# One encoder layer on one core: seam work moved between phases, scan copies placed earlier, one attention product put ahead of a barrier

## The chip, the cores and the metric

The kernel runs on one core of a Trainium2 chip (trn2). The metric is the device time of one execution in microseconds, as a median of runs. One further execution is profiled; all rows below are from it.

## The reference, cut to what matters

One layer over 1024 tokens of width 1024, in float32:

```python
h = h + 0.5 * swiglu(rmsnorm(h, ffn1_norm), w_gate, w_up, w_down)      # D_FF = 2816
n = rmsnorm(h, mix_norm); z = n @ w_in       # c_q 256 | c_kv 128 | k_rope 32 | u 512 | g_attn 1024 | g_ssm 1024
attn = mla_attention(...)                    # 8 heads, 64 + 32 rotary dims, latents c_q and c_kv, softmax over 1024 keys
ssm  = glu(gelu(s5_forward(u) + s5_backward(u) + d * u))               # 32 groups, 64 complex states, both directions
h = h + (sigmoid(g_attn) * (attn @ w_o_attn) + sigmoid(g_ssm) * (ssm @ w_o_ssm)) @ w_out
h = h + 0.5 * swiglu(rmsnorm(h, ffn2_norm), w2_gate, w2_up, w2_down)
out = rmsnorm(h, final_norm)
```

## The kernel before, in words

Each float32 operand of a large product is split into a rounded high part and a low rest, and each product is three matmul passes (high by high, high by low, low by high: lines 48 to 50, `three_passes`). So nearly every weight tile costs a cast on ScalarE (`high`) and a subtraction on VectorE or GpSimd (`low`) before TensorE can use it. The program is written out by hand: in each phase every engine has its own block of instructions in a fixed order, with explicit semaphore waits, and between two phases stands a barrier of all engines at which the old phase's semaphores are cleared (line 69). All DMAs of these phases are issued by SyncE and go through one queue (q1).

The phases, in order, are: first FFN, input projection, `ssm_phase`, `mixer_phase`, `merge_phase`, second FFN.

**The FFNs** (`ffn_phase`). The products are computed with seven block products in place of eight (`PRODUCTS`), so both the normalised rows and the weights are first combined into sums. The start of the phase, for matrix 0: TensorE turns the low rows (`turn_lows`, line 1314), makes `first_product` (0,0), then (0,2), turns the sums of one tile (`turn_sums`), makes `first_product` (1,0), turns the next sums, and so on, then goes on with product q = 1 of matrix 0. `T[i]`, the sums of rows, are made by GpSimd (`combine`, four instructions a tile), the weight sums `S` as well (`sums`, line 1300). `low` (line 1036) is VectorE's half of a weight block, `lows_low` and `sums_low` (lines 1065 and 1070) its halves of the turned rows, `normalised(i)` the root mean square of two tiles (`norm.var`, `norm.inverse`: five small instructions, lines 98 to 102) and the scaling of these tiles (line 1052). In the second FFN the first four tiles come normalised from the merge (`ahead=QUAD`); the other four are squared, stored to `kept` and normalised here. The first FFN has the same code without that head start.

**`ssm_phase`.** VectorE runs a serial scan of 127 steps, three small instructions each (lines 1758 to 1762). Beside it TensorE makes thirteen gate products `side.gp.product(pe, n)`, 48 matmuls each. `side.sigmoid(act, n)` reads the result of product n (line 1587), frees its PSUM banks, and casts the weights of product n + 2 (`gp.high(act, n + 2)`, line 165), from which GpSimd makes the low part (line 173), without which product n + 2 does not start. When the scan is over, `forward(b)` copies states on ScalarE (line 1711, two copies each) and `backward(b)` on VectorE, and TensorE makes the output product of block 0 (line 1683). ScalarE's order is:

```python
def forward(b):
    if b == 0:
        act.wait_ge(s["scan"], CH)          # the last step of the scan
...
for n in range(GATES_FIRST - 1):            # GATES_FIRST = 13
    side.sigmoid(act, n)
forward(0)
forward(1)
side.sigmoid(act, GATES_FIRST - 1)
```

**`mixer_phase`.** Eight products of the GLU (`glu.product(pe, n)`), after each of which one latent tile is turned (`latent(n)`, read by ScalarE and VectorE, lines 2112 and 2219), then the first head's projection (`project(0, x)`, which waits for all eight latents), then eight products with `w_o_ssm` (`wos.product`), after each of which one value tile is made (`value(n)`); then the loop over heads. VectorE evicts `wos` product n with line 2265; TensorE's product n + 2 waits for that. The last work of the heads is GpSimd's `aT_lo` (line 2330).

**`merge_phase`.** Eight products `woa.product(pe, n)` with `w_o_attn`, 24 matmuls each. VectorE's line 2466 multiplies product n with its gate tile (512 KB, loaded by line 2412 from DRAM), and product n + 2 waits for this read. SyncE issues gate 0, partial 0, weights 3, gate 1, partial 1, weights 4, then the 4 MB of `kept` (line 2416), and then, each after VectorE's sum n - 2, gate n, partial n and the next weights. Sixteen units with `w_out` follow, and at the end four residual additions by VectorE (line 2402).

Of the kernel before, what the change touches and what calls it, by code (L numbers as in the profile page):

```python
# [32 lines left out]
P = 128  # L33
# [662 lines left out]
def ffn_map(base):  # L696
# [5 lines left out]
    return where, total  # L702


def ffn_phase(nc, tag, gain, w_gate, w_up, w_down, rows, ident, psum, hidden, residual, x=None, finish=None, tables=None, ahead=0, following=None, loaded=None):
# [10 lines left out]
    with Phase(nc) as ctx:  # L716
# [6 lines left out]
        stat = sb("stat", [P, 5, ST])  # L723
        B_hi, B_lo = (at(n, [P, PRODUCTS, KH, HALF], F32R, n) for n in ("B_hi", "B_lo"))
        A_hi, A_lo = (at(n, [P, PRODUCTS, KH, P], F32R, n) for n in ("A_hi", "A_lo"))
        raw, gb = loaded or ([at(f"raw{j}", [P, KT, 2 * P], F32, "raw", 8 * KB * j) for j in range(2)], at("gb", [P, D], F32, "ring"))
        S = at("S", [P, 4, KH, P], F32, "S")
# [33 lines left out]
        s_kept = [sem(f"kept{m}") for m in range(ST if x is None else 0)]  # L761
# [22 lines left out]
        low_turned = lambda m, i: QUAD * i + m + 1  # L784
        arrived = lambda n: 32 * (n // 2 + (0 if loaded else 1))
# [13 lines left out]
        def _(sp):  # L799
# [17 lines left out]
            def take(m):  # L817
                if m < ahead:
                    return
                if x is not None:  # L820
                    sp.dma_start(rows[:, m, :], x[m * P:(m + 1) * P, :]).then_inc(s_x[m], 16)
                else:
                    sp.dma_start(residual[m * P:(m + 1) * P, :], rows[:, m, :]).then_inc(s_kept[m], 16)
# [68 lines left out]
        def _(act):  # L892
            def square(m):
                if x is not None:
                    act.wait_ge(s_x[m], 16)
                if m > ahead:
                    act.wait_ge(s_sq, m - ahead)
                act.activation(dump[:], rows[:, m, :], ACT.Square, accum_out=stat[:, 0, m:m + 1]).then_inc(s_sq, 1)  # L898

            def squares(i):  # L900
                square(2 * i)
                square(2 * i + 1)
                norm.root(act, i - ahead // 2, slice(2 * i, 2 * i + 2))
# [6 lines left out]
            def sums_high(m):  # L910
                if m == 0:
                    act.wait_ge(s_sq, ST - ahead)
# [8 lines left out]
            def high(n, q):  # L921
# [7 lines left out]
                if summed:  # L929
                    act.wait_ge(s_sum, 4 * n + summed)  # L930
                elif arrived(n):
# [50 lines left out]
            if not loaded:  # L982
                high(0, 0)
            squares(2)
# [3 lines left out]
            squares(3)  # L988
            high(1, 0)
            high(1, 2)  # L990
            sums_high(0)
# [4 lines left out]
            for q in (1, 3, 4, 5, 6):  # L996
# [42 lines left out]
        def _(dve):  # L1039
            def rstd(i):  # L1040
                norm.inverse(dve, i - ahead // 2, slice(2 * i, 2 * i + 2))

            def variance(i):
                dve.wait_ge(s_sq, 2 * i + 2 - ahead)
                norm.var(dve, i - ahead // 2, slice(2 * i, 2 * i + 2))

            def scaled(m):
                if m == 0:
                    dve.wait_ge(s_gain, 16)
                if x is None:  # L1050
# [49 lines left out]
            if not loaded:  # L1100
# [9 lines left out]
            for q in (1, 3, 4, 5, 6):  # L1110
# [164 lines left out]
        def _(pool):  # L1275
# [13 lines left out]
            def sums(n, part=slice(0, 4)):  # L1289
# [4 lines left out]
                for i, (a, b, op, q) in list(enumerate(((A21, A22, ALU.add, 4), (S[:, 0], A11, ALU.subtract, 1),  # L1294
# [3 lines left out]
                    if i in (1, 3):  # L1298
                        pool.wait_ge(s_sum, 4 * n + (1 if i == 1 else 2))
                    pool.tensor_tensor(S[:, i], a, b, op).then_inc(s_sum, 1)  # L1300

            sums(0)
# [296 lines left out]
def ssm_phase(nc, w, rows, rows_at, ident, psum, nT_hi, nT_lo, u, gates, kern_dram, C_dram, lam8_dram):  # L1599
# [5 lines left out]
    with Phase(nc) as ctx:  # L1605
# [83 lines left out]
        def _(act):  # L1689
# [29 lines left out]
            forward(0)  # L1719
            forward(1)  # L1720
# [871 lines left out]
```

## Time and profile before

| | us |
|---|---|
| median of 3 runs | 2269.32 |
| lowest, highest | 2269.16, 2269.6 |
| the profiled execution, its own time | 2267.31 |
| its span in the profile | 2265.5 |

TensorE was busy for 2144.2 us of the span (95%), VectorE for 1473.9, ScalarE for 916.9, GpSimd for 610.1. The granted TensorE clock was 0.982 of full speed in the mean: 1.00 is the level of 2.4 GHz, 0.50 that of 1.2 GHz. A time in a row of the timeline is counted from the start of the span. What stands in square brackets at the end of a row is the idle time of the engine before it, and who ended it.

### The profile page before, as it was taken

The page shows a single profiled execution, that of the slowest core. Times are in us where ns is not written, and L with a number is a line of the kernel's source. Part 1 is how long each engine was busy: PE and PEld are TensorE (multiplying, and loading weights), DVE is VectorE, ACT ScalarE, POOL GpSimd, SP SyncE. Part 2 cuts the span into 40 slices and gives each one's busy share as a digit, 9 for nine tenths or more (in the row PEclk, how much of TensorE's full clock was granted, in tenths as well). Part 3 has the DMA queues.
Part 4 walks back from the last instruction along what each step waited for, and adds up shares of the span by engine and source line. Part 5 has one row for each costly group of instructions (what it writes and reads, how often), then busy time and mean ns, then how long its engine had stood idle before and what let it go on. Part 6 is the DMA issues. An engine that isn't in the chain of part 4 may idle for free. (4 is left out here: it accounts for less than half of the span.)

```text
span 2265.5 us, 27670 instructions
## 1 busy us (share of the span) xinstructions
PE 2144.2 (95%) x10074; PEld 1779.3 (79%) x10074; DVE 1473.9 (65%) x2306; ACT 916.9 (40%) x1552; POOL 610.1 (27%) x510
## 2 busy tenths in 40 slices
PE   5899999999999899999999999899799999999997
PEld 4678888887887798878777887687678888887886
DVE  7786667657777524992447887454766565657777
ACT  5423333323445234225427778422533323324444
POOL 5337777750000003220002333100633333310000
PEclk9999999999999899999999999999899999999999
DMA  3433333349333427331340000362123232349333
GB/s 121 108 90 114 126 118 123 118 160 342 117 98 116 139 80 163 98 89 57 112 140 16 7 7 15 140 234 105 56 88 122 89 121 89 121 142 356 100 96 110
DMA packets 234471, 263.00 MB, mean 116 GB/s; under 512 B 34720, under 2 KB 169376, under 8 KB 233824
## 3 DMA queue, kind: packets, MB, share of 16 engines
q1 hardware_dynamic: 234336, 261.23, 36.4%
q8 instruction: 81, 1.33, 0.2%
q14 instruction: 54, 0.44, 0.1%
HBM read 184.60 MB, written 76.58 MB: 115 GB/s over the span
## 5 line engine op out<-in xcount | busy, mean ns | idle before, releaser
L48 PE MATMUL psum<-f_B_hi,f_A_hi 128*128 128x512 f32 x1232 | 489.8, 398 | 32.2 <-DVE f_A_lo L1036 23.7
L49 PE MATMUL psum<-f_B_lo,f_A_hi 128*128 128x512 f32 x1232 | 484.5, 393 | 0.0
L50 PE MATMUL psum<-f_B_hi,f_A_lo 128*128 128x512 f32 x1232 | 484.2, 393 | 0.0
L48 PEld LDWEIGHTS psum<-f_B_hi,f_A_hi 128*128 128x128 f32 x1232 | 234.2, 190 | 84.9 <-DVE f_A_lo L1036 27.5
L50 PEld LDWEIGHTS psum<-f_B_hi,f_A_lo 128*128 128x128 f32 x1232 | 234.2, 190 | 49.8
L49 PEld LDWEIGHTS psum<-f_B_lo,f_A_hi 128*128 128x128 f32 x1232 | 234.4, 190 | 47.6
L1300 POOL TENSOR_TENSOR f_S<-f_raw 128x512 f32<-128x512 f32 x88 | 134.7, 1531 | 445.5 <-DVE f_A_lo L1036 289.7
L933 ACT CAST f_A_hi<-f_S 128x512 fp32r<-128x512 f32 x176 | 109.2, 623 | 351.5 <-PE psum L50 347.1
L48 PE MATMUL psum<-f_wd,f_hh 128*128 128x512 f32 x616 | 240.4, 390 | 3.6 <-DVE f_wd L1082 3.6
L49 PE MATMUL psum<-f_wd,f_hh 128*128 128x512 f32 x616 | 240.4, 390 | 0.0
L50 PE MATMUL psum<-f_wd,f_hh 128*128 128x512 f32 x616 | 240.2, 390 | 0.0
L967 ACT CAST f_hh<-f_h_raw 128x512 fp32r<-128x512 f32 x154 | 96.0, 624 | 240.4 <-PE psum L50 231.7
L1036 DVE TENSOR_TENSOR f_A_lo<-f_raw,f_A_hi 128x512 fp32r<-128x512 f32 x132 | 132.4, 1004 | 70.1 <-ACT f_A_hi L933 69.4
L1080 DVE TENSOR_TENSOR f_hh<-f_h_raw,f_hh 128x512 fp32r<-128x512 f32 x154 | 106.6, 692 | 104.9 <-ACT f_hh L967 104.1
L1036 DVE TENSOR_TENSOR f_A_lo<-f_S,f_A_hi 128x512 fp32r<-128x512 f32 x176 | 138.7, 790 | 1.3 <-ACT f_A_hi L933 0.2
L933 ACT CAST f_A_hi<-f_raw 128x512 fp32r<-128x512 f32 x132 | 81.9, 620 | 142.1 <-PE psum L50 130.2
L48 PEld LDWEIGHTS psum<-f_wd,f_hh 128*128 128x128 f32 x616 | 116.0, 188 | 28.7 <-DVE f_wd L1082 4.4
L50 PEld LDWEIGHTS psum<-f_wd,f_hh 128*128 128x128 f32 x616 | 116.0, 188 | 24.2
L49 PEld LDWEIGHTS psum<-f_wd,f_hh 128*128 128x128 f32 x616 | 115.9, 188 | 23.9
L2211 DVE TENSOR_TENSOR mx_PT_lo<-psum,mx_PT_hi 128x512 fp32r<-128x512 f32 x128 | 87.8, 686 | 47.2 <-ACT mx_PT_hi L2076 46.8
L1737 POOL TENSOR_TENSOR u<-u,ss_C_mat 128x512 f32<-128x512 f32 x8 | 9.9, 1273 | 356.7 <-DMA ss_C_mat<-ssm_d 356.7
L1082 DVE TENSOR_TENSOR f_wd<-f_wd_raw,f_wd 128x512 fp32r<-128x512 f32 x154 | 105.7, 686 | 0.0
(327 smaller groups left out, 4277.3 us busy)
## 6 DMA issues: line engine op xcount, KB each, us to landing
f_h_raw<-hidden SPq DMA_DIRECT2D x154, 256.0 KB, 2.6
hidden<-rows SPq DMA_DIRECT2D x44, 768.0 KB, 4.6
f_raw<-ffn_w_gate SPq DMA_DIRECT2D x44, 512.0 KB, 5.1
f_raw<-ffn_w_up SPq DMA_DIRECT2D x44, 512.0 KB, 5.1
f_wd_raw<-ffn_w_down SPq DMA_DIRECT2D x44, 512.0 KB, 9.2
rows<-x SPq DMA_DIRECT2D x16, 512.0 KB, 7.3
ga_raw<-w_in SPq DMA_DIRECT2D x16, 512.0 KB, 4.3
gates<-ga_sig SPq DMA_DIRECT2D x32, 256.0 KB, 2.2
```

Source lines behind the costliest of these rows:

```text
L48: pe.matmul(out, lhs_hi, rhs_hi, start=first, stop=False, skip_group_check=go_on)
L49: pe.matmul(out, lhs_hi, rhs_lo, start=False, stop=False, skip_group_check=go_on)
L50: return pe.matmul(out, lhs_lo, rhs_hi, start=False, stop=last, skip_group_check=go_on)
L933: act.copy(A_hi[:, q], src).then_inc(s_hi, 1)
L967: act.copy(hh[v % 2][0][:], h_raw[v % 8][:]).then_inc(s_dhi, 1)
L1036: eng.tensor_tensor(A_lo[:, q], src, A_hi[:, q].bitcast(F32), ALU.subtract).then_inc(s_lo, 1)
L1080: dve.tensor_tensor(hh[v % 2][1][:], h_raw[v % 8][:], hh[v % 2][0][:].bitcast(F32), ALU.subtract).then_inc(s_dlo, 1)
L1082: dve.tensor_tensor(wd[v % 2][1][:], wd_of(q, k), wd[v % 2][0][:].bitcast(F32), ALU.subtract).then_inc(s_dlo, 1)
L1300: pool.tensor_tensor(S[:, i], a, b, op).then_inc(s_sum, 1)
L1737: pool.tensor_tensor(u[:, g], u[:, g], Db[:, g].unsqueeze(2).broadcast_to([P, 4, T, SG]), ALU.mult).then_inc(s["ud"], 1)
L2211: dve.tensor_tensor(pt(PT_lo, g, x), turned_bank(x), pt(PT_hi, g, x).bitcast(F32), ALU.subtract).then_inc(s["tr_lo"], 1)
```

## The change

It has five parts.

1. `ssm_phase`: on ScalarE `forward(0)` and `forward(1)` stand after `side.sigmoid(act, 8)` in place of after `side.sigmoid(act, 11)`. What `forward(0)` waits for is the same.
2. `mixer_phase`: latent 1 is turned together with latent 0 after GLU product 0, and each later one a product sooner, the last after product 6; ScalarE and VectorE take a pair of latents directly after the sigmoid, ahead of the casts of the weights and of the wait for the next product. The value tiles are moved in the same way.
3. `woa.product(pe, 0)` is the last work of TensorE in `mixer_phase`, where it waits for the parts of `aT_lo` as it needs them; `merge_phase` starts with product 1.
4. The squares of tiles 4 to 6, the stores of tiles 4 to 7 and the four weight sums of matrix 0 are made in `merge_phase`. The second FFN squares tile 7 alone, normalises the four tiles with one chain of small instructions and scales tiles 6 and 7 later.
5. In both FFNs `high(0, 1)` and `low(0, 1)` stand ahead of the sums' halves (`sums_high`, `sums_low`) in place of behind them.

The diff, cut to its core:

```diff
 # ffn_phase, ScalarE
-            squares(2)
+            if loaded:
+                square(ST - 1)
+                norm.root(act, 0, slice(QUAD, ST))
+            else: ...
             lows_high(1)
             high(0, 2)
             first_copy(0)
-            squares(3)
+            if not loaded:
+                squares(3)
             high(1, 0)
             high(1, 2)
+            high(0, 1)
             sums_high(0)
...
-            for q in (1, 3, 4, 5, 6):
+            for q in (3, 4, 5, 6):
                 high(0, q)
 # ffn_phase, VectorE
-            normalised(2)
+            if loaded:
+                dve.wait_ge(s_sq, SQUARES)
+                norm.var(dve, 0, slice(QUAD, ST))
+                norm.inverse(dve, 0, slice(QUAD, ST))
+                scaled(QUAD)
+                scaled(QUAD + 1)
...
             lows_low(1)
             low(0, 2)
-            normalised(3)
+            if loaded:
+                scaled(QUAD + 2)
+                scaled(QUAD + 3)
...
             low(1, 0)
             low(1, 2)
+            low(0, 1)
             for m in range(QUAD):
                 sums_low(m)
 # ffn_phase, GpSimd
-            sums(0)
+            if not loaded:
+                sums(0)
 # ssm_phase, ScalarE
             for n in range(GATES_FIRST - 1):
                 side.sigmoid(act, n)
-            forward(0)
-            forward(1)
+                if n == GATES_FIRST - 5:
+                    forward(0)
+                    forward(1)
             side.sigmoid(act, GATES_FIRST - 1)
 # mixer_phase
+        def sooner(n):
+            return (0, 1) if n == 0 else (n + 1,) if n + 1 < ST else ()
...
             for n in range(glu.N):
                 glu.product(pe, n, (lambda k: pe.wait_ge(s_lo, 2 * k + 2)) if n == 0 else None)
-                latent(n)
+                for m in sooner(n):
+                    latent(m)
...
                 wos.product(pe, n, (lambda k: pe.wait_ge(s_vlo, k + 1)) if n == 0 else None)
-                value(n)
+                for m in sooner(n):
+                    value(m)
...
+            pe.wait_ge(s["exp"], G)
+            woa.product(pe, 0, lambda k: pe.wait_ge(s["av_lo"], 4 * k + 4))
 # merge_phase, SyncE, ScalarE, GpSimd, TensorE
-            sp.wait_ge(s_next, 64)
+            for i in range(QUAD):
+                sp.wait_ge(s_add, QUAD + i + 1)
+                sp.dma_start(kept[(QUAD + i) * P:(QUAD + i + 1) * P, :], rows[:, QUAD + i, :]).then_inc(s_keep[QUAD + i], 16)
...
+            for m in range(QUAD, ST - 1):
+                act.wait_ge(s_add, m + 1)
+                act.wait_ge(s_sq, m)
+                act.activation(dump[:], rows[:, m, :], ACT.Square, accum_out=next_stat[:, 0, m:m + 1]).then_inc(s_sq, 1)
...
+            pool.wait_ge(s_next[0], 32)
+            pool.tensor_tensor(next_S[:, 0], A21, A22, ALU.add).then_inc(s_nsum, 1)
...
-            for n in range(KT):
+            for n in range(1, KT):
                 woa.product(pe, n)
```

How the instructions stand now, at three places. The first is ScalarE in `ssm_phase`, around the copies of states (`rows<-ss_H`); a row `ga_sig` is one sigmoid, `ga_hi` the cast of the weights of the product after the next. Before:

```order
L165 CAST ga_hi<-ga_raw 128x1024
L1587 ACTIVATE ga_sig<-psum 128x512 x2
L165 CAST ga_hi<-ga_raw 128x1024
L1711 COPY rows<-ss_H 64x128x8 x4
L1587 ACTIVATE ga_sig<-psum 128x512 x2
L165 CAST ga_hi<-ga_raw 128x1024
L1711 COPY rows<-ss_H 64x128x8 x2
```

And of the changed kernel, on the same engine:

```order
L165 CAST ga_hi<-ga_raw 128x1024
L1731 COPY rows<-ss_H 64x128x8 x4
L1607 ACTIVATE ga_sig<-psum 128x512 x2
L165 CAST ga_hi<-ga_raw 128x1024
L1607 ACTIVATE ga_sig<-psum 128x512 x2
L165 CAST ga_hi<-ga_raw 128x1024
L1607 ACTIVATE ga_sig<-psum 128x512 x2
L165 CAST ga_hi<-ga_raw 128x1024
L1607 ACTIVATE ga_sig<-psum 128x512 x2
L165 CAST ga_hi<-ga_raw 128x1024
L1731 COPY rows<-ss_H 64x128x8 x2
```

The four copies of blocks 0 and 1 stood one sigmoid and one cast ahead of the next two copies, and now stand four of each ahead of them.

The second place is the end of `mixer_phase` on TensorE (the branches are the end of one phase's block and the start of the next one's; `mx_PT_lo,mx_V` is the last product of the heads). Before:

```order
L1987 MATMUL psum<-mx_PT_hi,mx_V 128x512
L1988 MATMUL psum<-mx_PT_lo,mx_V 128x512
L1792 UNCONDITIONAL_BRANCH
L2497 UNCONDITIONAL_BRANCH
L48 MATMUL psum<-aT_hi,woa_hi 128x512
```

And of the changed kernel, with the first and the last of the product's 24 matmuls:

```order
L2012 MATMUL psum<-mx_PT_hi,mx_V 128x512
L2013 MATMUL psum<-mx_PT_lo,mx_V 128x512
L48 MATMUL psum<-aT_hi,woa_hi 128x512
...
L50 MATMUL psum<-aT_hi,woa_lo 128x512
L1813 UNCONDITIONAL_BRANCH
L2549 UNCONDITIONAL_BRANCH
L48 MATMUL psum<-aT_hi,woa_hi 128x512
```

Product 0 stands ahead of the branches, so ahead of the barrier.

The third place is VectorE at the start of the second FFN. Before, from the halves of the first turned rows on:

```order
L1065 TENSOR_TENSOR f_B_lo<-psum,f_B_hi 128x4x128 x4
L1036 TENSOR_TENSOR f_A_lo<-f_raw_15743,f_A_hi 128x512
L368 TENSOR_SCALAR f_stat<-f_stat 128x2
L98 RECIPROCAL f_stat<-f_stat 128x2
L99 TENSOR_TENSOR f_stat<-f_stat 128x2
L100 TENSOR_TENSOR f_stat<-f_stat 128x2
L101 TENSOR_SCALAR f_stat<-f_stat 128x2
L102 TENSOR_TENSOR f_stat<-f_stat 128x2
L1052 SCALAR_TENSOR_TENSOR rows<-rows,f_stat,f_gb 128x1024 x2
L1036 TENSOR_TENSOR f_A_lo<-f_raw_15744,f_A_hi 128x512 x2
L1070 TENSOR_TENSOR f_B_lo<-psum,f_B_hi 128x4x128 x20
L1036 TENSOR_TENSOR f_A_lo<-f_S,f_A_hi 128x512 x3
```

And of the changed kernel, the same stretch:

```order
L1073 TENSOR_TENSOR f_B_lo<-psum,f_B_hi 128x4x128 x4
L1044 TENSOR_TENSOR f_A_lo<-f_raw_15774,f_A_hi 128x512
L1060 SCALAR_TENSOR_TENSOR rows<-rows,f_stat,f_gb 128x1024 x2
L1044 TENSOR_TENSOR f_A_lo<-f_raw_15775,f_A_hi 128x512 x2
L1044 TENSOR_TENSOR f_A_lo<-f_S,f_A_hi 128x512
L1078 TENSOR_TENSOR f_B_lo<-psum,f_B_hi 128x4x128 x20
L1044 TENSOR_TENSOR f_A_lo<-f_S,f_A_hi 128x512 x2
```

The second chain of small instructions is gone (one chain of twice the width stands earlier), and one half of the weight sums has moved ahead of the twenty halves of the turned sums.

## Rows read from the trace of the kernel before

**Rows 1.** The page, part 1: busy time, share of the span, instructions.

```profile
PE 2144.2 (95%) x10074; PEld 1779.3 (79%) x10074; DVE 1473.9 (65%) x2306; ACT 916.9 (40%) x1552; POOL 610.1 (27%) x510
```

**Rows 2.** Timeline of ScalarE in `ssm_phase`: start us, us, instruction, idle before it.

```profile
972.54 1.05 ACT L165 CAST ga_hi<-ga_raw 128x1024 fp32r<-128x1024 f32 x1
982.45 1.09 ACT L1587 ACTIVATE ga_sig<-psum 128x512 f32<-128x512 f32 x2 [8.86 <-PE psum L50]
...
993.33 1.09 ACT L1587 ACTIVATE ga_sig<-psum 128x512 f32<-128x512 f32 x2 [8.86 <-PE psum L50]
...
1015.00 7.40 ACT L1711 COPY rows<-ss_H 64x1024 f32<-64x1024 f32 x4 [8.77 <-DVE ss_H L1762]
...
1023.21 1.03 ACT L165 CAST ga_hi<-ga_raw 128x1024 fp32r<-128x1024 f32 x1
```

**Rows 3.** Timelines of GpSimd and VectorE in `ssm_phase`.

```profile
1024.32 2.41 POOL L173 TENSOR_TENSOR ga_lo<-ga_raw,ga_hi 128x1024 fp32r<-128x1024 f32 x1 [15.61 <-ACT ga_hi L165]
984.64 2.38 DVE L1762 TENSOR_TENSOR ss_H<-ss_H,ss_prod 128x64 f32<-128x64 f32 x1
...
1014.74 0.22 DVE L1762 TENSOR_TENSOR ss_H<-ss_H,ss_prod 128x64 f32<-128x64 f32 x1
```

**Rows 4.** Timeline of TensorE, the output products of blocks 0 and 1.

```profile
1018.92 5.44 PE L1683 MATMUL psum<-ss_C_mat,rows 128*128 128x128 f32 x32 [3.87 <-ACT rows L1711]
...
1035.12 3.73 PE L1683 MATMUL psum<-ss_C_mat,rows 128*128 128x128 f32 x32
```

**Rows 5.** Timelines of TensorE, VectorE and ScalarE in `mixer_phase`, ahead of the heads.

```profile
1132.47 0.79 PE L48 MATMUL psum<-mx_lT_hi,mx_w_hi 128*128 128x512 f32 x1 [4.21 <-DVE mx_lT_lo L2219]
...
1189.83 0.47 PE L48 MATMUL psum<-mx_KT_hi,mx_QT_hi 96*128 96x512 f32 x1 [1.49 <-DVE mx_V L2223]
1130.25 1.22 DVE L2246 TENSOR_TENSOR mx_sT_lo<-mx_val,mx_sT_hi 128x1024 fp32r<-128x1024 f32 x1 [1.11 <-ACT mx_sT_hi L2137]
...
1162.20 1.23 DVE L2265 TENSOR_TENSOR mx_out<-psum,mx_gate 128x1024 f32<-128x1024 f32 x1
...
1135.43 0.59 ACT L2058 ACTIVATE mx_qf<-psum 64x512 f32<-64x512 f32 x1 [3.66 <-PE psum L50]
```

**Rows 6.** Timelines of GpSimd, TensorE, SyncE's queue and VectorE around the merge's start.

```profile
1448.65 1.26 POOL L2330 TENSOR_TENSOR aT_lo<-mx_att,aT_hi 64x512 fp32r<-64x512 f32 x1 [0.81 <-ACT aT_hi L2107]
1451.14 0.77 PE L48 MATMUL psum<-aT_hi,woa_hi 128*128 128x512 f32 x1 [6.12 <-PEq L69]
1454.02 0.54 SPq L2416 DMA_DIRECT2D rows<-kept  x1
1461.77 0.33 SPq L2412 DMA_DIRECT2D mg_gate<-gates  x1
...
1473.63 1.23 DVE L2466 TENSOR_TENSOR mg_val<-psum,mg_gate 128x1024 f32<-128x1024 f32 x1 [4.72 <-DMA mg_gate<-gates]
```

**Rows 7.** Windows there: us, busy of each engine, granted clock, DMA share, GB/s.

```profile
1451.14:1456.25 5.11, 5.11 (x12) 4.05 (x13) 0.00 (x0) 0.00 (x0) 0.00 (x0) 0.50 0.79 263
1462.00:1473.20 11.20, 11.20 (x51) 9.29 (x50) 4.53 (x5) 2.50 (x3) 0.00 (x0) 1.00 1.03 405
```

**Rows 8.** Timelines of TensorE and VectorE at the second FFN's start.

```profile
1598.77 0.79 PE L48 MATMUL psum<-f_B_hi,f_A_hi 128*128 128x512 f32 x1 [4.91 <-DVE f_A_lo L1036]
1610.29 0.79 PE L48 MATMUL psum<-f_B_hi,f_A_hi 128*128 128x512 f32 x1 [4.35 <-DVE f_A_lo L1036]
1627.45 0.80 PE L48 MATMUL psum<-f_B_hi,f_A_hi 128*128 128x512 f32 x1 [2.87 <-DVE f_A_lo L1036]
1604.99 3.58 DVE L1052 SCALAR_TENSOR_TENSOR rows<-rows,f_stat,f_gb 128x1024 f32<-128x1024 f32 x2
...
1626.71 1.89 DVE L1036 TENSOR_TENSOR f_A_lo<-f_S,f_A_hi 128x512 fp32r<-128x512 f32 x3
```

**Rows 9.** TensorE at the first FFN's start; ScalarE's square there in the second.

```profile
59.23 0.50 PE L48 MATMUL psum<-f_B_hi,f_A_hi 128*128 128x512 f32 x1 [2.87 <-DVE f_A_lo L1036]
1589.11 1.09 ACT L898 ACTIVATE f_dump<-rows 128x1024 f32<-128x1024 f32 x1
```

More of the change, by code:

```diff
@@ L760, in ffn_phase @@
         s_gain, s_sq, s_xn, s_T, s_tr, s_bhi, s_blo = map(sem, ("gain", "sq", "xn", "T", "tr", "bhi", "blo"))
-        s_kept = [sem(f"kept{m}") for m in range(ST if x is None else 0)]
+        if loaded:
+            ctx.taken += loaded[4].taken
+        s_kept = loaded[5] if loaded else None
+        SQUARES = 1 if loaded else ST
         s_raw = [sem(f"raw_in{j}") for j in range(2)]
@@ L895, in square @@
                     act.wait_ge(s_x[m], 16)
-                if m > ahead:
-                    act.wait_ge(s_sq, m - ahead)
+                if m and not loaded:
+                    act.wait_ge(s_sq, m)
                 act.activation(dump[:], rows[:, m, :], ACT.Square, accum_out=stat[:, 0, m:m + 1]).then_inc(s_sq, 1)
@@ L902, in squares @@
                 square(2 * i + 1)
-                norm.root(act, i - ahead // 2, slice(2 * i, 2 * i + 2))
+                norm.root(act, i, slice(2 * i, 2 * i + 2))
             def lows_high(i):
@@ L928, in high @@
                     act.wait_ge(s_tr, ALL_TURNED)
-                if summed:
-                    act.wait_ge(s_sum, 4 * n + summed)
-                elif arrived(n):
+                if summed and sums_done(n, summed):
+                    act.wait_ge(s_sum, sums_done(n, summed))
+                elif not summed and arrived(n):
                     act.wait_ge(s_raw[j], arrived(n))
@@ L981, in _ @@
             lows_high(0)
-            if not loaded:
+            if loaded:
+                square(ST - 1)
+                norm.root(act, 0, slice(QUAD, ST))
+            else:
                 high(0, 0)
-            squares(2)
+                squares(2)
             lows_high(1)
@@ L2150, in _ @@
                         queries(0, x)
-                value(n)
+                for m in sooner(n):
+                    value(m)
             split(1)
@@ L2266, in _ @@
                 wos.low(dve, n + 3)
-                value(n)
+                for m in sooner(n):
+                    value(m)
                 if n == 1:
@@ L2552, in build @@
         where, _ = ffn_map(-(-nc.sbuf_base // 32) * 32)
+        stores = Taken()
         loaded = ([nc.alloc_sbuf_tensor_at(f"f2_raw{j}", [P, KT, 2 * P], F32, offset=where["raw"] + 8 * 1024 * j) for j in range(2)],
-                  nc.alloc_sbuf_tensor_at("f2_gb", [P, D], F32, offset=where["ring"]))
+                  nc.alloc_sbuf_tensor_at("f2_gb", [P, D], F32, offset=where["ring"]),
+                  nc.alloc_sbuf_tensor_at("f2_S", [P, 4, KH, P], F32, offset=where["S"]),
+                  nc.alloc_sbuf_tensor_at("f2_stat", [P, 5, ST], F32, offset=where["stat"]),
+                  stores, [semaphores(nc, stores, "keep")(f"tile{m}") for m in range(ST)])
         merge_phase(nc, w, psum, rows, kept, woa, held, loaded, gates, partial, w["ffn2_norm"][0])
```

59 lines of the change are left out of this document (38 added, 21 removed).

## The prediction

> **What bounds the kernel now.** First the page's busy times: TensorE is busy for 95% of the span [rows 1], so only what shortens one of its waits, or a stretch at the low clock, can make the kernel faster, and any new wait of TensorE is paid in full. So next I listed TensorE's waits in the timeline, and for each the engine that ended it. The five parts of the change aim at six of them: 3.87 us at the scan's end [rows 4], 4.21 and 1.49 us in the mixer [rows 5], 6.12 us at the merge's start [rows 6], and 4.91, 4.35 and 2.87 us at the second FFN's start [rows 8], with a 2.87 us wait in the first FFN that is like the last of these [rows 9]. After each of the longer ones TensorE restarts at half clock: 5.11 us at 0.50 behind the 6.12 us wait [rows 7], first matmuls of 0.79 us behind the others [rows 5, 8]. At half clock half of the time is lost, 2.55 us in the first case; in the mixer the six matmuls of the first projection took 1135.43 - 1132.47 = 2.96 us [rows 5] where six at full clock take 1.36 (48 take 993.33 - 982.45 = 10.88 us [rows 2]), so 1.6. For a restart that I can't place I take 2.3 us, a little outside these two as bounds: 1.5 to 2.9.
>
> **Part 1, the scan's copies: a wait that blocks ScalarE.** The copies wait for the scan's last step, which ends at 1014.96 [rows 3], and the copies' row says so: 8.77 us idle, ended by VectorE's `ss_H` [rows 2]. They are not held up by the sigmoids ahead of them; ScalarE is idle there. In the new order ScalarE comes to them after the cast of 972.54 [rows 2] and stands still until the scan is over. Behind it is queued sigmoid 9, at 982.45 before, and its cast. That cast makes the weights of product 11, and sigmoid 9 frees the banks that product 11 writes. Product 10 still runs, as its cast is the one of 972.54. It ends where the sigmoid of 993.33 begins [rows 2], and there TensorE stops.
>
> How long it stops: the scan itself gets shorter, since GpSimd's subtraction blocks one step of it each time: a step's instruction that takes 0.22 us takes 2.38 beside GpSimd's 2.4 [rows 3]. Three of these subtractions (those behind the sigmoids 9, 10 and 11) now come after the scan: 3 x 2.16 = 6.5 us, so it ends at 1008.5. The copies take 7.40 [rows 2], to 1015.9. From the copies' end (1022.40) to the end of GpSimd's next low part (1024.32 + 2.41 = 1026.73) it is 4.33 us [rows 2, 3]; by the same steps product 11 starts at 1020.2. TensorE is idle for 1020.2 - 993.3 = 26.9 us, and restarts at half clock, 2.3 more. Then the products 11 and 12 run back to back, as before; the copies are long done, so the 3.87 us wait is gone, and the output product of block 0 runs at full clock (3.73 in place of 5.44, 1.7 less [rows 4]). Sum: 26.9 + 2.3 - 3.87 - 1.7 = **+23.6 us** (bounds 22 to 25: the restart's, and one blocked step more or less).
>
> **Part 2, latents and values.** Latent 7 is now turned before the last GLU product and read while that runs, so the projection starts where the product ends: the 4.21 us go, and with them the half clock (1.6). TensorE is then 5.8 us earlier. What is late next is ScalarE's read of the projection (1135.43 before): it waits also for VectorE's last `sT_lo`, whose end stays at 1131.47, so it comes 3.9 us sooner and not 5.8. From it a chain over VectorE's rotary instructions, the eviction of `wos` product 0, a weight load, ScalarE's queries and a value leads to the eviction of 1162.20 [rows 5], for which product 4 waits; it moves by the same 3.9, and TensorE waits about 2 us there. The 1.49 us wait for the last value goes too, as that value stands before the last product now, and so does a little of its three matmuls (0.7 us) from behind it: 3.9 + 1.49 + 0.3 = **-5.7 us** (bounds -3.9, the chain alone, and -7.3, all of 4.21, 1.6 and 1.49).
>
> **Part 3, the attention product.** Its 24 matmuls take 5.44 us at full clock (half of 10.88 [rows 2]). 18 of them need parts of `aT_lo` that are there, and run in the idle stretch that begins at 1451.14 - 6.12 = 1445.02. The last six wait for GpSimd's 1448.65 + 1.26 = 1449.91 [rows 6] and end at about 1451.45. The barrier took 1.23 us from 1449.91 to 1451.14; it now ends at about 1452.7, so everything that SyncE issues for the merge is 1.55 us later. TensorE has product 0 behind it and no half clock, and runs products 1 to 3 (3 x 5.44) until 1469.05. Before, it reached product 4 at 1451.14 + 4 x 5.44 + 2.55 = 1475.45. But product 4 waits for VectorE's read of product 2, which waits for gate 2, and this landed only just before 1473.63, issued at 1461.77: 4.72 us of idle, ended by the DMA [rows 6]. Ahead of it in the queue stand the 4 MB of `kept`, issued at 1454.02; the DMA engines are full from then on (share 1.03 at 405 GB/s [rows 7]). A faster TensorE does not make these bytes come sooner, and they start 1.55 us later. So VectorE's read is at 1475.2 to 1476.4, and TensorE waits from 1469.05 to 1476.4, 7.4 us, then restarts at half clock (2.3). Against 1475.45 that is 0.95 + 2.3 = **+3.2 us** (bounds 2.4 to 3.9, the restart's), and products 5 to 7 follow.
>
> The Trainium skill, DMA: Bandwidth & Descriptors, section Queues, rings and completion order, says that descriptors are consumed in ring order on each DMA engine, but that completion is not first in, first out per issuing engine. If gate 2 could overtake `kept`, part 3 would give what its idle time promises (the second rival). Here the trace is for the order of issue: gate 2 came 19.6 us after `kept` was issued and not before it.
>
> **Part 4, the second FFN's start.** The stores in the merge add a last DMA issue behind the last addition, 0.33 to 0.54 us of SyncE [rows 6], to the barrier: +0.4. The squares of tiles 4 to 6 run beside the additions of the next tiles, the weight sums on GpSimd beside the units, at no cost (if they were not hidden, one square, 1.09 [rows 9]). At the start one square is gone from the chain to the first wait and VectorE no longer meets GpSimd's sums: 4.91 becomes 3.9, -1.0. In the second wait, TensorE stood for VectorE's second norm: from 1598.7 to 1608.57, ahead of `low(1, 0)` [rows 8]. Now two scalings alone stand there, at most 3.58, while TensorE makes product (0,2) and turns a tile for over 7 us: the 4.35 us go, and the half clock behind them (1.5, the low bound, as turns of rows follow soon). In the third wait `low(0, 1)` is ready, so TensorE need not wait for one of the three in 1.89 us [rows 8], nor for the last of the twenty halves, as long again, which product q = 1 does not read: -1.2. Sum 0.4 - 1.0 - 4.35 - 1.5 - 1.2 = **-7.6 us**. What is late next is GpSimd's row sums, four tiles in series. Bounds: -4.5, if those hold the third turn up by 3 us, and -10, if a restart or two keeps the full clock.
>
> **Part 5, the first FFN.** The same 1.2 us of the wait of 59.23 [rows 9]: **-1.2 us** (bounds 0 and -2.9, with the half clock behind it).
>
> **Sum.** 23.6 - 5.7 + 3.2 - 7.6 - 1.2 = +12.3 us. The profiled execution took 2267.31 by its own clock, 1.8 around a span of 2265.5, and would take 2279.6. It lies 2.0 below the median of 2269.32, to which I add the same: **2281.6 us**.
>
> **The rivals.**
> *The scan's wait costs nothing* (other side, faster). If the scan were over when ScalarE comes to the copies, the copies would lie in its idle time (8.86 us beside each product [rows 2]), and part 1 would give -3.87 - 1.7 = -5.6. Sum -16.9: 2252.4. The point from which part 1 decides the sign: its cost must be under 11.3, so the scan must end 12.3 us earlier than 1008.5, at 996. VectorE's rows show no such slack; for it is only that part 1 was meant so. 0.03.
> *`kept` does not bind.* Then TensorE keeps part 3's gain: 5.44 of product 0 and 2.55 of half clock, less 1.55: -6.4 in place of +3.2. 2272.0. For it is that the queue might serve small loads sooner, against it the row of the gate. 0.07.
> *The row sums bind at the second FFN.* GpSimd's instructions and VectorE's meet more than before, as the scalings and three halvings stand in one run; part 4 gives its low bound or less, -3: 2286.2. 0.12.
> My forecast, all five parts within their bounds: 0.78.
>
> **How the numbers follow.** Faster than before by over 0.2% (4.5 us; about what a measurement of this kernel tells from no change) is below 2264.8, slower is above 2273.8. Faster needs the first rival: 0.03, and 0.01 for a sum of mistakes. Within lie the second rival and the low tail of the forecast, 0.08. Slower: 0.88. The bounds of the five terms, added in squares about the sum, are some 4 us to either side; the low end goes further, to take in most of what the second rival leaves out: 2275.5 to 2287.
>
> **What the changed profile would show.** Right: a wait of TensorE of about 27 us in `ssm_phase` ahead of product 11, released by `ga_lo`, and ScalarE idle for some 35 us ahead of the copies, released by `ss_H`; no wait ahead of the first projection, but one of about 2 us ahead of a `wos` product; a new wait of about 7 us among the `woa` products, ended by VectorE's `mg_val` that itself waits for the gate's DMA, with clock 0.50 behind it; of the waits at the second FFN's start one of about 3.9 us, and none of 4.35. Wrong would be: copies that run before 1000 us, or products 11 and 12 without a wait; product 4 of the merge before 1475; a first product q = 1 of the second FFN over 38 us after its phase's start (now 40.95, predicted 33).

## The result and the profile after

| | before | changed |
|---|---|---|
| median, 5 runs each | 2269.6 us | 2280.84 us |
| lowest, highest | 2269.16, 2271.57 | 2280.62, 2282.77 |
| the profiled execution, and its span | 2267.31, 2265.5 | 2280.62, 2278.6 |

The ratio is 1.005, with a 95% interval of 1.0038 to 1.0063: the change makes the kernel 11 us slower, where 12.3 were forecast. By the two spans it is 13.1 us.

The page of the changed kernel, part 1 (busy us, share of the span, instructions), answers to [rows 1]:

```profile
PE 2140.6 (94%) x10074; PEld 1775.5 (78%) x10074; DVE 1469.8 (65%) x2300; ACT 916.9 (40%) x1551; POOL 610.9 (27%) x510
```

TensorE is busy for 3.6 us less in a span that is 13.1 longer: it waits 16.7 us more. To find the place, the program is cut at the first instruction of TensorE in each stage, as the timeline gives its start, and the differences are taken (us); the mixer's stage is cut once more, at the first matmul of the heads' scores (`mx_KT`, `mx_QT`). Each row is one profiled execution. The experiments stand in the same table; what each of them is follows below.

| kernel | first FFN | projection | `ssm_phase` | mixer up to the first scores | heads and merge | second FFN |
|---|---|---|---|---|---|---|
| before | 729.4 | 114.1 | 228.8 | 117.6 | 396.7 | 679.0 |
| changed | 725.7 | 114.3 | 253.1 | 111.8 | 402.8 | 670.9 |
| 1: copies back | 724.9 | 114.0 | 228.7 | 111.9 | 402.6 | 672.5 |
| 2: product 0 back | 726.0 | 115.1 | 252.4 | 111.5 | 399.2 | 670.9 |
| 3: `kept` split | 724.8 | 114.3 | 253.0 | 112.0 | 393.1 | 671.0 |
| 4: split, product 0 back | 726.1 | 114.3 | 251.7 | 113.4 | 399.6 | 672.5 |
| 5: copies and latents back | 725.1 | 114.3 | 228.7 | 117.6 | 401.7 | 670.9 |
| 6: FFN parts only | 725.6 | 114.3 | 228.7 | 117.6 | 400.5 | 672.5 |
| 7: part 5 only | 727.4 | 115.2 | 230.0 | 118.0 | 399.4 | 680.8 |
| 8: three edits | 724.9 | 114.0 | 225.7 | 111.9 | 393.1 | 671.0 |
| 9: later subtraction | 725.7 | 113.9 | 225.8 | 111.8 | 402.3 | 672.5 |
| 10: still later | 725.3 | 115.5 | 226.7 | 113.4 | 402.3 | 671.0 |
| 11: three edits, still later | 724.6 | 115.5 | 225.1 | 112.0 | 393.2 | 670.9 |

`ssm_phase` takes 24.3 us more, the heads and the merge 6.1 more; the mixer's start takes 5.8 less, the second FFN 8.1 less, the first 3.7 less, in these two executions. A stage with the same code can differ by 2 to 3 us between two executions: heads and merge, which experiment 7 leaves alone, took 399.4 us there against 396.7 before. Now the places themselves. Timelines of the changed kernel in `ssm_phase` (start us, us, what; in brackets the idle time before): ScalarE, then VectorE, GpSimd and TensorE. They answer to [rows 2 to 4].

```profile
969.09 1.06 ACT L165 CAST ga_hi<-ga_raw 128x1024 fp32r<-128x1024 f32 x1
1005.11 7.34 ACT L1731 COPY rows<-ss_H 64x1024 f32<-64x1024 f32 x4 [34.97 <-DVE ss_H L1783]
1012.26 1.10 ACT L1607 ACTIVATE ga_sig<-psum 128x512 f32<-128x512 f32 x2
1013.25 1.03 ACT L165 CAST ga_hi<-ga_raw 128x1024 fp32r<-128x1024 f32 x1
...
1004.85 0.23 DVE L1783 TENSOR_TENSOR ss_H<-ss_H,ss_prod 128x64 f32<-128x64 f32 x1
...
1014.36 2.34 POOL L173 TENSOR_TENSOR ga_lo<-ga_raw,ga_hi 128x1024 fp32r<-128x1024 f32 x1 [41.73 <-ACT ga_hi L165]
...
1016.75 0.79 PE L48 MATMUL psum<-nT_hi,ga_hi 128*128 128x512 f32 x1 [26.91 <-POOL ga_lo L173]
...
1041.50 3.73 PE L1703 MATMUL psum<-ss_C_mat,rows 128*128 128x128 f32 x32
```

The chain is read from bottom to top. Product 11 waits 26.91 us for GpSimd's low part. This waited for ScalarE's cast of 1013.25, and the cast stood behind the copies. Ahead of the copies ScalarE was idle for 34.97 us, until the scan's last step, which ends at 1005.08. The phase itself starts 3.45 us earlier than in the kernel before; counted from there, the step ends at what would be 1008.5 in that kernel's rows. Block 0's output product now runs without a wait and at full clock.

TensorE and VectorE of the changed kernel in the mixer, against [rows 5]:

```profile
1180.99 0.47 PE L48 MATMUL psum<-mx_sT_hi,wos_hi 128*128 128x512 f32 x1 [2.76 <-DVE mx_out L2295]
...
1179.62 1.23 DVE L2295 TENSOR_TENSOR mx_out<-psum,mx_gate 128x1024 f32<-128x1024 f32 x1
```

The 4.21 and 1.49 us waits are gone; `wos` product 4 waits 2.76 us. TensorE, SyncE and VectorE at the merge's start, against [rows 6], then three windows against [rows 7], the first in the last head (us, busy of PE, PEld, DVE, ACT and POOL, granted clock, DMA share, GB/s):

```profile
1466.91 0.50 PE L48 MATMUL psum<-aT_hi,woa_hi 128*128 128x512 f32 x1 [0.90 <-POOL aT_lo L2361]
...
1469.76 0.47 PE L48 MATMUL psum<-aT_hi,woa_hi 128*128 128x512 f32 x1 [1.20 <-PEq L69]
...
1494.21 0.76 PE L48 MATMUL psum<-aT_hi,woa_hi 128*128 128x512 f32 x1 [7.84 <-DVE mg_val L2518]
...
1472.57 0.53 SPq L2447 DMA_DIRECT2D rows<-kept  x1
1475.92 1.14 SPq L2443 DMA_DIRECT2D mg_gate<-gates  x1
...
1481.27 6.17 SPq L2444 DMA_DIRECT2D mg_part<-partial  x1
...
1492.84 1.23 DVE L2518 TENSOR_TENSOR mg_val<-psum,mg_gate 128x1024 f32<-128x1024 f32 x1 [10.22 <-DMA mg_gate<-gates]
```
```profile
1456.39:1459.80 3.41, 3.41 (x12) 2.48 (x11) 0.00 (x0) 0.17 (x1) 1.31 (x2) 0.50 0.00 0
1472.60:1492.80 20.20, 13.77 (x61) 11.07 (x59) 7.33 (x7) 3.25 (x4) 0.00 (x0) 0.94 1.02 385
1494.21:1497.35 3.14, 3.14 (x8) 2.46 (x9) 3.14 (x4) 1.57 (x2) 0.00 (x0) 0.50 1.06 376
```

The wait of 6.12 us is 1.20, and one of 7.84 stands ahead of product 4. Gate 2, issued 3.35 us behind `kept`, let VectorE go on at 1492.84, 16.9 us after its issue, with the DMA engines full in between (share 1.02). Counted from the issue of `kept`, VectorE could read the gate after 20.3 us. In all nine profiles with one load of `kept` this took 18.9 to 20.3 us, whether gate 2 was issued 3.4 us behind `kept` (product 0 ahead of the barrier) or 6.8 to 8.1 us (product 0 behind it): to issue the gate sooner does not bring it sooner. The second FFN's start, TensorE and VectorE, against [rows 8], and TensorE in the first FFN, against [rows 9]:

```profile
1607.71 3.69 PE L1334 MATMUL psum<-ident,rows 128*128 128x128 f32 x32 [2.94 <-PEq L69]
...
1618.49 0.79 PE L48 MATMUL psum<-f_B_hi,f_A_hi 128*128 128x512 f32 x1 [3.89 <-DVE f_A_lo L1044]
...
1641.18 0.47 PE L48 MATMUL psum<-f_B_hi,f_A_hi 128*128 128x512 f32 x1 [1.19 <-DVE f_B_lo L1078]
...
1645.87 0.47 PE L48 MATMUL psum<-f_B_hi,f_A_hi 128*128 128x512 f32 x1 [1.72 <-DVE rows L1140]
...
1618.35 4.52 DVE L1060 SCALAR_TENSOR_TENSOR rows<-rows,f_stat,f_gb 128x1024 f32<-128x1024 f32 x2
...
58.22 0.47 PE L48 MATMUL psum<-f_B_hi,f_A_hi 128*128 128x512 f32 x1 [1.76 <-DVE f_B_lo L1078]
...
62.91 0.47 PE L48 MATMUL psum<-f_B_hi,f_A_hi 128*128 128x512 f32 x1 [1.68 <-DVE rows L1140]
```

The first product with q = 1 starts 33.5 us after the phase's first instruction (before 40.9). Of the three waits 3.89, none and 1.19 are left. A new one of 0.52 us, for GpSimd's row sums, stands ahead of the last turn of the sums, at 1639.34.

### The profile page after: what moved, and what is told of

Same layout as the page of the kernel before. It is cut to its first block and busy times, and to the rows that moved or that the text cites. A ratio compares the mean times of both kernels' runs of the same rounds, so it can differ in the third digit from the quotient of the medians.

```text
span 2278.6 us, 27668 instructions
## 1 busy us (share of the span) xinstructions
PE 2140.6 (94%) x10074; PEld 1775.5 (78%) x10074; DVE 1469.8 (65%) x2300; ACT 916.9 (40%) x1551; POOL 610.9 (27%) x510
## 5 line engine op out<-in xcount | busy, mean ns | idle before, releaser
L1319 POOL TENSOR_TENSOR f_S<-f_raw 128x512 f32<-128x512 f32 x86 | 129.2, 1502 | 302.8 <-DVE f_A_lo L1044 282.5
L48 PE MATMUL psum<-nT_hi,ga_hi 128*128 128x512 f32 x256 | 101.4, 396 | 27.8 <-POOL ga_lo L173 26.9
```

The source lines that it names most:

```text
L48: pe.matmul(out, lhs_hi, rhs_hi, start=first, stop=False, skip_group_check=go_on)
```

## The experiments

Each table row above is one profiled execution, and not always the one nearest to the median; the medians below are of 4 to 12 runs, each beside runs of the kernel before on the same chip, whose median was 2270.29 for the experiments 1 to 4, 2272.94 for 5 to 8 and 2271.83 for 9 to 11 (17, 17 and 11 runs). These three medians differ by up to 2.7 us with one and the same kernel, and the changed kernel was not run beside them. So a difference from its 2280.84, or between experiments of different groups, can be off by as much; the ratios and the stages don't depend on that. All but 7 start from the changed kernel.

**1. Part 1 undone.**

```diff
-                if n == GATES_FIRST - 5:
-                    forward(0)
-                    forward(1)
+            forward(0)
+            forward(1)
             side.sigmoid(act, GATES_FIRST - 1)
```

> The changed kernel with part 1 undone: the four copies of the scan's states stand behind sigmoid 11 again. Theory (the copies' wait for the scan blocks ScalarE, and this costs 26.9 of idle TensorE and 2.8 of restart, less the 3.87 wait and 1.6 of half clock that went): 24.3 us less than the changed kernel's 2280.84, so 2256.5, with a wait of about 3.9 ahead of the output product of block 0 and none ahead of product 11. Rival (the wait of 26.9 comes mostly from the earlier start of the phase and from what stands before it, and the place of the copies moves only the last 3.87): 2277 to 2285.

Measured: 2258.01 us (2256.59 to 2259.25), ratio 0.9946 (0.9933 to 0.9958). `ssm_phase` took 228.7 us in place of 253.1, what it took before; the wait ahead of block 0 is back, with a restart at half clock (5.44 in place of 3.73), and ahead of product 11 there is none. TensorE's timeline:

```profile
1014.25 5.44 PE L1703 MATMUL psum<-ss_C_mat,rows 128*128 128x128 f32 x32 [3.87 <-ACT rows L1731]
```

The place of two lines, the copies, costs 24.4 us, and it alone decides the sign of the change. The rival had 2277 to 2285 and is out.

**2. Product 0 back in the merge** (`woa.product(pe, 0, ...)` out of the heads' block, `for n in range(KT)` in the merge).

> The changed kernel with the first attention output product back in the merge, behind the barrier. Theory (product 0 ahead of the barrier makes everything that SyncE issues later, and gate 2 behind the 4 MB of kept sets the time of product 4): 3.4 us less than 2280.84, so 2277.4; 2275.7 if the half clock of the last head goes too; a wait of 6 at the barrier and none ahead of product 4. Rival (product 0 ahead saves its 5.44 and the half clock behind the barrier, and the 7.84 wait has nothing to do with it): 6.4 us more, 2287.2.

Measured: 2277.04 us (2275.71 to 2279.65), ratio 1.0031 (1.0019 to 1.0044). Heads and merge took 399.2, 3.6 less than with part 3. The barrier's wait is back, and ahead of product 4 there is none:

```profile
1467.95 0.76 PE L48 MATMUL psum<-aT_hi,woa_hi 128*128 128x512 f32 x1 [6.12 <-PEq L69]
```

The rival's 2287.2 is out. The last head has its half clock here too, so product 0 is not its cause.

**3. The load of `kept` in 8 pieces.** VectorE waits for the first four ahead of the first additions and for the others ahead of the last.

```diff
-                if n == 1:
-                    sp.dma_start(rows[:], kept.rearrange("(m p) d -> p m d", p=P)).then_inc(s_kept, 16)
+                if n >= QUAD:
+                    back(sp, n - QUAD)       # one tile of 512 KB
...
                 if 3 <= u < 7:
+                    back(sp, u + 1)
```

> The changed kernel with the 4 MB load of kept cut into 8 loads of 512 KB, one each behind the gates 4 to 7 and the weights of units 3 to 6, in place of one load behind gate 1. Theory (gate 2 lands late only because 4 MB stand ahead of it): the 7.84 us wait ahead of product 4 and the restart behind it, 2.4, go: 10.2 us less than 2280.84, so 2270.6, and gate 2 lands within 5 us of its issue. Rival (the DMA engines are the limit, whatever the order, as the same bytes must be moved in the same stretch): the wait stands a little later, 2279 to 2282.

Measured: 2270.95 us (2269.39 to 2273.59), ratio 1.0005 (0.9996 to 1.0014). TensorE has no wait between the barrier's and the end of the products. SyncE's queue and VectorE's reads of the products 2 and 3, and a window:

```profile
1475.06 0.32 SPq L2446 DMA_DIRECT2D mg_gate<-gates  x1
...
1480.99 1.23 DVE L2522 TENSOR_TENSOR mg_val<-psum,mg_gate 128x1024 f32<-128x1024 f32 x1 [0.64 <-DMA mg_gate<-gates]
1485.46 1.23 DVE L2522 TENSOR_TENSOR mg_val<-psum,mg_gate 128x1024 f32<-128x1024 f32 x1 [0.15 <-PE psum L50]
```
```profile
1472.00:1485.00 13.00, 13.00 (x59) 10.78 (x58) 11.22 (x11) 4.82 (x6) 0.00 (x0) 1.00 1.04 373
```

The DMA engines are as full as in the changed kernel (share 1.04 and 1.02), so the rival's premise holds, but its conclusion doesn't: the gate is read 5.9 us after its issue (within 5 was expected) in place of 16.9, because less stands ahead of it. Heads and merge took 393.1 in place of 402.8, 9.7 less.

**4. Both.**

> Both edits: product 0 back in the merge and kept in 8 loads. Theory (without product 0 ahead, gate 2 was in time by 1.8 us, so kept cost nothing there): the same as with product 0 back alone, 2277.4 (or 2275.7), so product 0 ahead of the barrier is worth 5 to 7 us once kept is out of its way, and costs 3.4 when it is not. Rival (kept slows other transfers of the merge in both cases): some 5 us less than with product 0 back alone, near 2271.

Measured: 2277.07 us (2275.69 to 2279.49), ratio 1.0029 (1.0018 to 1.0041), the same as experiment 2: without product 0 ahead, splitting `kept` gives nothing, and the rival (near 2271) is out. So the two edits are worth something only together: product 0 ahead costs 3.6 us behind the one load (402.8 - 399.2) and gives 6.5 behind the split one (399.6 - 393.1). The 3.6 are of one pair of executions: with one load of `kept`, the five profiles with product 0 ahead have 401.7 to 402.8 for the stage and the four experiments without it (2, 6 and 7, and 4 with its split load) 399.2 to 400.5, in the mean some 2.6 less.

**5. Parts 1 and 2 undone** (latents and values behind the product with their own number again).

> The changed kernel without the parts 1 and 2: copies behind sigmoid 11, latents and values at their old places; parts 3, 4 and 5 stay. Theory (part 2 is worth 5.7 us, and 5.8 by the marks of the two profiles): 2258.0, measured without part 1 alone, plus 5.7: 2263.7, with the 4.21 and 1.49 us waits back in the mixer. Rival (the half clock in the last head, 3.4 us long, which the kernel before does not have, comes from part 2 and takes 1.6 of its gain): 2262.1, and no half clock there.

Measured: 2263.61 us (2260.23 to 2266.01), ratio 0.9969 (0.9954 to 0.9984): 5.7 over experiment 1 by the stage (117.6 against 111.9), and 5.2 by the two ratios. The half clock in the last head is there without part 2, so the rival falls.

**6. Parts 1, 2 and 3 undone.**

> The changed kernel without the parts 1, 2 and 3: only what changes the two FFNs, their loads, stores, squares and weight sums. Theory (part 3 costs 3.4 us; the parts 4 and 5 give 7.3 and 3.4 by the marks): 2259 to 2260.5. Rival (the first FFN gives only the 1.2 us of one wait, the rest of its 3.4 was a difference of two executions): 2261.5 to 2263.

Measured: 2261.06 us (2257.43 to 2261.83), ratio 0.9948 (0.9936 to 0.996). Beside experiment 5, on the same chip, part 3 costs 2.6 us. The median lies 8.5 below the 2269.6 of the first table, and 11.9 below the runs of the kernel before beside it; the forecast for both FFN parts was 8.8. The two readings differ by more than theory (2259 to 2260.5) and rival (2261.5 to 2263), and the median lies between them, so this run doesn't tell them apart.

**7. Part 5 alone, on the kernel before** (it changes both FFNs).

```diff
             high(1, 2)
+            high(0, 1)
             sums_high(0)
...
-            for q in (1, 3, 4, 5, 6):
+            for q in (3, 4, 5, 6):
```

> The kernel before with one edit: in both FFNs matrix q = 1 is split directly behind (1, 2), ahead of the sums of tiles and weights. Theory (1.2 us of each of two waits of 2.87): 2.4 us less than before, 2267.2, and of the waits 1.7 is left. Rival (the first FFN's 3.4 us by the marks are this edit's): 3.4 there and 1.2 to 3.4 in the second, 2263 to 2265.

Measured: 2268.23 us (2264.14 to 2272.6, 12 runs), ratio 0.9984 (0.9974 to 0.9993): by the ratio 3.6 us less, with an interval of 1.6 to 5.9, and by the medians 4.7. The theory's 2.4 lies in the interval, and so does the near end of the rival's 4.6 to 6.8, so the size stays open. Both waits of 2.87 are 1.76. TensorE's timeline in the second FFN, which took 680.8 us against 679.0 all the same, as it has 6.8 us more at half clock in this execution (the slowest of the twelve):

```profile
1630.93 0.47 PE L48 MATMUL psum<-f_B_hi,f_A_hi 128*128 128x512 f32 x1 [1.76 <-DVE f_B_lo L1071]
```

Experiment 6 differs from this kernel by part 4 alone. On the same chip it is 7.2 us faster by the medians and 8.2 by the ratios; the forecast for part 4 without the 1.2 us of its third wait, which both kernels have, was 6.4.

**8. Three edits:** copies back, `kept` split, and GpSimd's subtraction for product 13 behind the scan.

```diff
             for n in range(1, side.N):
+                if n == GATES_FIRST:
+                    pool.wait_ge(s["scan"], CH)
                 side.gp.low(pool, n)
```

> The changed kernel with three edits: the copies behind sigmoid 11 again, kept in 8 loads, and GpSimd's subtraction for product 13 behind the scan's last step in place of beside it. Theory: 2258.0 measured without part 1, less 9.7 (the wait of 7.29 ahead of product 4 and a restart of 2.4), less 2.2 (one step of the scan no longer takes 2.4 in place of 0.22, so the scan ends 2.2 sooner and the wait of 3.87 ahead of block 0 becomes 1.7): 2246.1. Rival (the subtraction behind the scan comes too late for product 13, or VectorE's copies of the states meet it): no gain from this edit, 2248.3, or a new wait ahead of product 13, 2250.

Measured: 2251.83 us (2242.57 to 2252.19), ratio 0.9905 (0.989 to 0.9921). The five runs lie in two groups, 2242.57 and 2245.45, and three at 2251.83 to 2252.19: the median misses the 2246.1 of the theory, and the rival's 2248.3 as well. The profile is of the fastest run, so what the slower three have more is not shown. In it the wait ahead of block 0 was not 1.7 but 2.54. VectorE and GpSimd behind the scan:

```profile
1008.28 6.86 DVE L1791 COPY rows<-ss_H 64x1024 f32<-64x1024 f32 x4
...
1008.33 3.36 POOL L173 TENSOR_TENSOR ga_lo<-ga_raw,ga_hi 128x1024 fp32r<-128x1024 f32 x1 [15.12 <-DVE ss_H L1784]
```

VectorE's four copies took 6.86 us in place of 4.31, and the subtraction 3.36 in place of 2.4. The collision was moved, not removed, as the rival had it, though it took 0.8 of the expected 2.2 us and not all. The Trainium skill, SBUF — State Buffer, section Who interferes with whom, says that copies can lock the port pair that VectorE shares with GpSimd, and that the one that comes second stands still until the other's instruction is over; by it each loses about one instruction of the other, and the rows agree with 2.5 and 1.0 us.

**9 and 10. The subtraction behind the scan, and behind VectorE's copies** (`pool.wait_ge(s["bw"], 4)` in place of the wait above), both with the copies back and one load of `kept`.

> The copies behind sigmoid 11 again, and GpSimd's subtraction for product 13 waits for the scan's last step; kept is one load. Against the copies back alone (2258.0) theory says: the wait ahead of block 0 is 2.5 in place of 3.87, as in the run with all three edits, where the subtraction then ran beside VectorE's copies of the states and made four of them take 6.87 in place of 4.36; and the half clock behind this wait goes, 1.7: 3.0 less, 2255.0. Rival (the half clock was gone by chance of the execution): 1.3 less and the half clock is there, 2256.7.

> As the run before, but GpSimd's subtraction waits for VectorE's four copies of the states too. Theory (an instruction of VectorE that reads and writes SBUF takes longer beside GpSimd's): the four copies take 4.4 again, ScalarE's first two are then what block 0 waits for, 1.7 in place of 2.5, and product 13 is not late, as the subtraction ends near 1015.1 and product 13 starts near 1016.0: 0.8 less than the run before, 2254.2. Rival (product 13 waits for the subtraction): a new wait of 1 to 2 there, and no gain, 2255 to 2256.5.

Measured: 2256.81 us (2253.89 to 2260.08), ratio 0.9938 (0.9925 to 0.9951), and 2256.1 us (2252.73 to 2257.83), ratio 0.9931 (0.9917 to 0.9944). The two medians are 0.7 apart, with runs that spread over 5 to 6 us, and so don't tell the two apart. TensorE and VectorE in the profiles, first of 9, then of 10:

```profile
1013.75 3.81 PE L1703 MATMUL psum<-ss_C_mat,rows 128*128 128x128 f32 x32 [2.59 <-DVE rows L1791]
...
1009.00 6.86 DVE L1791 COPY rows<-ss_H 64x1024 f32<-64x1024 f32 x4
```
```profile
1014.24 4.99 PE L1703 MATMUL psum<-ss_C_mat,rows 128*128 128x128 f32 x28 [1.89 <-ACT rows L1731]
...
1010.19 4.67 DVE L1791 COPY rows<-ss_H 64x1024 f32<-64x1024 f32 x4
```

With the subtraction behind the copies these are short again and ScalarE is the one that is waited for: 1.89 in place of 2.59. But the shorter wait has a restart at half clock behind it (28 of the 32 matmuls take 4.99 us; at full clock all 32 take 3.81), and the longer one has none. So the stage took 225.8 us in experiment 9 and 226.7 in 10. The theory's waits were right in both, and no wait ahead of product 13 came, as the rival of 10 had it; but the gain of 0.8 was not seen. For 9 the profile, of the fastest of six runs, has what the theory says, no half clock, while the median of 2256.81 is the number of its rival (2256.7), by which the half clock goes only in some executions. Experiment 10, where it is back behind a shorter wait, speaks for that rival.

**11. The three edits with the later subtraction.**

> The three edits together, with the subtraction behind VectorE's copies: copies behind sigmoid 11, kept in 8 loads. Theory: 2254.2 less 9.7: 2244.5. Rival (some of the restarts come back elsewhere, as in the first such kernel, whose executions lay between 2242.6 and 2252.2): median 2248 to 2251.

Measured: 2244.08 us (2242.94 to 2245.94, 4 runs), ratio 0.9883 (0.9867 to 0.9899). The theory had 2244.5, the rival 2248 to 2251. This is 1.2% below the kernel before and, by medians that were not taken side by side, 1.6% below the changed one (2244.08 / 2280.84). Its `ssm_phase` took 225.1, its heads and merge 393.2. Block 0 in TensorE's timeline:

```profile
1013.55 3.81 PE L1703 MATMUL psum<-ss_C_mat,rows 128*128 128x128 f32 x32 [1.92 <-ACT rows L1731]
```

The wait is that of experiment 10, and here no half clock follows it.

## Why the prediction was right

The median was forecast at 2281.6 and is 2280.84; the span at 2277.8 (2265.5 + 12.3) and is 2278.6. The mechanisms were those forecast, and the experiments 1 to 4 show the two that matter. That the total is within 1 us is in part luck: two differences of 2.5 us that no term had, more in heads and merge and less in the first FFN, cancel (the last two points below).

- **Part 1, +23.6; measured +24.4** (253.1 against 228.7 with the copies back). The scan's end (1008.5) and the wait of 26.9 us were right to 0.1. What is missing is the restart, taken at 2.3: TensorE's distance to the kernel before grew from 23.6 us at the first matmul of product 11 to 26.4 behind it, so 2.8. That three blocked steps would go from the scan was rightly read from one row: from the phase's start to the scan's end it is 165.05 us in place of 171.48, 6.4 less where 6.5 was said.
- **Part 2, -5.7; measured -5.7** (experiment 5 against 1, by the stage). The new wait is 2.76 and not 2: 0.85 us stood there before, and the 1.9 us by which it grew are the difference of 5.8 and 3.9 that the working has. The term was right, the wait in the last part misnamed.
- **Part 3, +3.2; measured +3.6, and 2.6 by the medians** of the experiments 5 and 6. The wait was 7.84 where 7.4 stood (7.06 to 7.32 in the four other profiles with the same order). Two errors partly cancel in it. Against experiment 2, product 4 starts 2.0 us later in the stage (289.3 us after its start in place of 287.3), where 0.95 was worked out. The restart behind costs 1.6 (half of the 3.14 us at 0.50), where 2.3 was taken. The cause is shown from both sides: product 0 back takes the wait away, and so does splitting `kept`. The rival in which `kept` does not bind had 6.4 us as the gain of part 3; with `kept` out of the way it is 6.5. The order of the queue was the right thing to doubt, and it decides.
- **Part 4, -7.6.** By the stages the second FFN took 8.1 less, of which 0.75 is given back at the barrier ahead of it (2.94 in place of 2.19, where 0.4 was said): 7.3. Experiment 6 against 7 has 7.2 by the medians for what 6.4 was forecast. The waits came as foretold, 3.89, none, 1.19, and the mark at 33.5 where 33 was said (its "now 40.95" is 40.92 in the rows). So at the mark 7.45 us were gained and not 8.05; the rest came just behind it, where the half clock behind the third wait went too, which the sum leaves out, and the next wait grew from 0.93 to 1.72. One bound failed: the two scalings took 4.52 us, with GpSimd's row sums beside them, and not at most 3.58. It cost nothing, since TensorE had over 7 us of work. The row sums themselves did bind, but for 0.52 us and not for 3: the rival in which they bind was nearer than it looked.
- **Part 5, -1.2.** 1.11 us of the 2.87 wait went, and the product behind it starts 1.0 us sooner (58.22 against 59.23). The stage as a whole took 3.7 less, but the same code took 724.6 to 727.4 us in twelve profiles, against one of 729.4 before; in the one changed profile the next wait is 1.68, and 3.41 us less are spent at half clock, the stretch behind this wait. In the experiments 4 and 7 that stretch is there all the same, so its absence can't be put down to the edit. Experiment 7 has 1.6 to 5.9 for both FFNs, where this term and the same in part 4 say 2.4. The one wait is shown; how much of the rest is the edit's stays open.
- **Heads and merge, 6.1 in the table against 3.2 + 0.4.** The remaining 2.5 us are the barrier's further 0.35, the 0.4 by which part 3 was undersized, and the half clock in the last head (3.41 us, of which 1.7 are lost), which the profile of before doesn't have. All eleven experiments have it too, 7 among them, whose heads and merge are those of the kernel before, so it belongs to no part; why the one profile of before was without it stays open.

The first rival (the scan's wait costs nothing) is answered by experiment 1: with the copies at their old place the other four parts give 11.6 us (2269.6 - 2258.01; 12.3 against the runs beside it), so the sign hung on part 1 alone, as was said.

## What to carry to other kernels

Moving an instruction ahead in an engine's order moves its wait ahead too: look up what releases it in the trace, and if it is late, everything queued behind it inherits the delay (here 7 us of copies, moved up by three sigmoids, made 27 us of idle TensorE). An engine that is given its work sooner gains only until the next transfer it needs, so before filling an idle stretch list the loads that come next and what stands ahead of them in the queue; one large load cut into pieces behind the small urgent ones turned a loss of 3.6 us into a gain of 6.5. Test such edits in pairs, since each alone showed nothing or a loss.

## What the hardware showed beyond that

- **A restart at half clock doesn't follow from the length of the wait alone.** Ahead of block 0's product TensorE waited 1.89, 1.92 and 2.59 us in the experiments 10, 11 and 9. Their code of this stage is the same but for one wait of GpSimd, and in 10 and 11 the same altogether. Behind the 1.89 it ran at half clock, behind the other two at full (all 32 matmuls in 3.81 us).
- **Executions of one kernel differ by such stretches.** The second FFN from its first instruction took 670.9 to 671.0 us or 672.5 us with the same code, a step of 1.6. In experiment 4 the step is half of one more stretch of 3.41 us at 0.50, in the middle of the stage. In 1, 6 and 9 the first 32 turns run at half clock (6.60 to 6.65 us in place of 3.69), and a shorter first wait (2.9 to 3.0 us in place of 3.9) gives back part of it. The five runs of experiment 8 were 2242.57, 2245.45, 2251.83, 2251.85 and 2252.19 us, at mean granted clocks of 0.987, 0.985, 0.983, 0.983 and 0.982. An edit worth 1 us can't be read from a median of some five runs here; in the timeline the wait that it removes can be read, but not what it is worth over many runs.
- **Issuing a DMA can hold up the engine that issues it.** In the changed kernel SyncE's issue of partial 3, with `kept` in the queue, took 6.17 us where the three before it took 0.42 to 0.51. It took 5.5 to 6.5 us in all five profiles that have product 0 ahead of the barrier and one load of `kept`, and 0.43 to 1.55 in the four with product 0 behind it. Here nothing urgent stood behind it.
